# Third layer's mixer: gate and value pairs projected first, convolution ahead of queries and keys, taps between attention steps

## Chip, core and metric

The kernel runs on one core of one Trainium2 chip. The time is the device time of one execution in microseconds (us), from the first to the last instruction of the program. TensorE does the matrix products and writes to PSUM (eight banks); ScalarE, VectorE read PSUM and work on SBUF; SyncE issues the weight transfers. The trace calls them PE (with PEld for the loading of stationary operands), ACT, DVE and SP.

## What is computed

Three transformer layers run one after the other on 256 positions of width 1024, all in float32. The first two are of one kind and are not touched. The third is this, cut to what matters:

```python
def hybrid_mixer(h, w_in, b_f, conv_w, conv_b, conv_ln_g, conv_ln_b, w_o):
    proj = h @ w_in                       # q 512, k 512, v 512, f 8, value 512, gate 512
    log_f = jax.nn.log_sigmoid(f_logit + b_f)
    attn = fox_attention(q, k, v, log_f)  # 8 heads; logits + cum[t] - cum[s], causal softmax
    u = conv_val * jax.nn.sigmoid(conv_gate)
    u = causal_depthwise_conv(u, conv_w, conv_b)      # 31 taps, 512 channels
    u = jax.nn.silu(layer_norm(u, conv_ln_g, conv_ln_b))
    return jnp.concatenate([attn, u], axis=-1) @ w_o

    # around it: mod = silu(c) @ ada_w + ada_b gives shift, scale and gate (sh, sc, g) of mixer and FFN
    #   h = rms_norm(x, pre_g) * (1 + sc) + sh;  x = x + g * rms_norm(mixer or FFN of h, post_g)
```

## The kernel before

**Units.** All weights pass through one list, `UNITS`. A unit is 1 MB of weights: 256 output columns of a projection (for `f`, 128 columns). SyncE loads it into one of six `raw` buffers; ScalarE copies it, rounded, to `w_hi`; VectorE subtracts to get `w_lo` (the split, three buffers each); TensorE then makes three products for each pair of blocks (hi by hi, lo by hi, hi by lo), 48 matmuls of 256 columns for a unit. The split of unit m waits until unit m-3 is done on TensorE. ScalarE and VectorE each walk the list by hand: `step()` moves to the next unit, `split_ahead()` splits the one three further on, `tick()` does both, `unit_in()` waits until TensorE is done with the unit at hand. All engines run their instructions strictly as the code is written; semaphores (`Event`, `wait_ge`) tie them together.

**PSUM.** Results of units go to four banks in rotation (`plan_banks`), and a unit waits until the bank's last user has been evacuated by ScalarE or VectorE. Four more banks (`A`, "steps" in the trace) hold attention, sums and the FFN's output.

**Third layer.** The first two units, `gate0` and `val0`, are multiplied with the not yet normalised x (`x_shifted`) and scaled when VectorE evacuates them (`shifted_evac`); the reciprocal root `rs` comes from `norm_sum(4)` and ScalarE. Then `normalise(4)` on VectorE and `normed_hi(4)` on ScalarE make `h_hi` and `h_lo` for all other units. `modulation(1)`, 24 products of one column each (48 matmuls in the trace), makes the last three vectors of `mod`; its results are needed for `gain` from the end of the mixer on. The units followed as f, q0, q1, k0, k1, v0, v1, gate1, val1, out0 to out3, then the FFN's: gate, up and down in turn.

**Convolution.** Of its four chunks of 128 channels, 0 to 2 are done on VectorE tap by tap (`conv(taps, chunks)`, 31 taps, `conv_acc` in the trace), chunks 0 and 1 in alternation and chunk 2 alone. Chunk 3 is done on TensorE by 31 matmuls with diagonal matrices (`last_chunk`, 62 in the trace), which ScalarE builds (`diagonals(n)`, eight at a time). Chunks 0 and 1 need gate0 and val0; 2 and 3 need gate1 and val1.

**Attention** goes in two blocks of 128 queries, `first` and `second`, generators that are advanced with `next`: logits on TensorE, maxima on VectorE (`row_max`), exponentials on ScalarE (`probs`), transposes of `probs` on TensorE, copies on ScalarE (`probsT`), products with v, scaling to `y_tm` on VectorE, transposes again, and the split into `ya_hi` and `ya_lo`. Their logits wait for all of k and for `c_rows`, the running sums of the forget gate.

**FFN start.** `feed_forward(2)`: gate unit 0 and up unit 0 are again multiplied with `x_shifted` and evacuated with `shifted_evac`; gate unit 1 takes the bank that gate unit 0 had.

## Time and profile before

| | |
|---|---|
| median of 3 executions | 1255.02 us (1252.8 to 1255.05) |
| the profiled execution | 1247.75 us, span 1246.0 us |
| TensorE busy | 1172.1 us, 94% of the span, mean granted clock 0.975 |
| VectorE busy | 846.0 us, 68% |
| ScalarE busy | 614.9 us, 49% |
| DMA | 214.15 MB, mean 172 GB/s |
| third layer's mixer (from its first unit) | 872.95 to about 1021 us |

TensorE's share is an average: it is nearly full in the FFNs and has its idle pieces between the stages. The whole change lies between 880 and 1066 us of the span.

### The profile page before, as it was taken

How to read it: one execution, taken by the hardware profiler on the slowest of the kernel's cores; microseconds unless marked ns; L12 is line 12 of the kernel's file. 1: busy time of each engine (PE TensorE's matmuls, PEld its weight loads, DVE VectorE, ACT ScalarE, POOL GpSimd, SP SyncE). 2: the span in 40 equal slices, each digit the busy share in tenths (PEclk: the TensorE clock that was granted, in tenths of full speed). 3: DMA queues.
4: the chain of work that ended last, by engine and by line, in shares of the span. 5: the costliest groups of instructions: out<-in, count | busy, mean ns of one | idle time of the engine just before them, and what ended most of it. 6: DMA issues, size and time to landing. Idle time of an engine off the chain costs nothing.

```text
span 1246.0 us, 21102 instructions
## 1 busy us (share of the span) xinstructions
PE 1172.1 (94%) x9014; PEld 1135.4 (91%) x9014; DVE 846.0 (68%) x1270; ACT 614.9 (49%) x738; POOL 0.2 (0%) x4
## 2 busy tenths in 40 slices
PE   5999999999999999999999999999989787999996
PEld 4799899999999988999899999999889687999996
DVE  6995565777686779946567776768596747444453
ACT  7675347454433365653465534333594365433433
POOL 0000000000000000000000000000000000000000
PEclk9999999999999989999999999999799898999998
DMA  9446343747676744543347378867353122555511
GB/s 346 149 153 199 107 135 102 244 162 259 231 262 233 271 140 135 172 152 119 101 136 250 125 269 270 281 228 222 98 182 102 56 102 73 178 190 171 195 42 34
DMA packets 177614, 214.15 MB, mean 172 GB/s; under 512 B 3696, under 2 KB 160752, under 8 KB 177520
## 3 DMA queue, kind: packets, MB, share of 16 engines
q1 hardware_dynamic: 176800, 211.86, 51.4%
q8 instruction: 71, 1.16, 0.4%
q10 hardware_dynamic: 720, 0.94, 0.2%
q14 instruction: 23, 0.19, 0.0%
HBM read 211.74 MB, written 1.05 MB: 171 GB/s over the span
## 4 chain that ended last, share of the span: by engine, by line
PE 70%; DVE 17%; ACT 9%; issue 2%; DMA 1%; SPq 0%; DVEq 0%; ACTq 0%
PE stream L494 15%; PE stream L495 15%; PE stream L496 15%; DVE w_lo L1341 7%; PE steps L496 4%; PE steps L495 4%; PE steps L494 4%; ACT w_hi L907 4%; PE steps L825 2%; PE steps L683 1%; PE stream L702 1%; PE stream L608 1%; DMA raw<-in_w_in 1%; DVE score L1478 1%; PE steps L673 1%
## 5 line engine op out<-in xcount | busy, mean ns | idle before, releaser
L1341 DVE TENSOR_TENSOR w_lo<-raw,w_hi 128x2048 fp32r<-128x2048 f32 (+2 forms) x178 | 402.5, 2266 | 253.5 <-ACT w_hi L907 252.7
L907 ACT ACTIVATE w_hi<-raw 128x2048 fp32r<-128x2048 f32 (+2 forms) x178 | 336.4, 1893 | 357.8 <-PE stream L496 315.3
L494 PE MATMUL stream<-h_hi,w_hi 128*128 128x256 f32 x1576 | 451.1, 286 | 13.3 <-DVE w_lo L1341 9.5
L495 PE MATMUL stream<-h_lo,w_hi 128*128 128x256 f32 x1576 | 447.6, 284 | 0.0
L496 PE MATMUL stream<-h_hi,w_lo 128*128 128x256 f32 x1576 | 447.5, 284 | 0.0
L494 PEld LDWEIGHTS stream<-h_hi,w_hi 128*128 128x128 f32 x1576 | 304.1, 193 | 16.0 <-DVE w_lo L1341 11.0
L495 PEld LDWEIGHTS stream<-h_lo,w_hi 128*128 128x128 f32 x1576 | 304.2, 193 | 0.6 <-issue 0.5
L496 PEld LDWEIGHTS stream<-h_hi,w_lo 128*128 128x128 f32 x1576 | 303.9, 193 | 0.0
L494 PE MATMUL steps<-gu_hi,w_hi 128*128 128x256 f32 x528 | 149.6, 283 | 0.7 <-DVE gu_lo L1601 0.7
L496 PE MATMUL steps<-gu_hi,w_lo 128*128 128x256 f32 x528 | 149.5, 283 | 0.0
L495 PE MATMUL steps<-gu_lo,w_hi 128*128 128x256 f32 x528 | 149.5, 283 | 0.0
L494 PEld LDWEIGHTS steps<-gu_hi,w_hi 128*128 128x128 f32 x528 | 101.4, 192 | 0.9 <-issue 0.9
L496 PEld LDWEIGHTS steps<-gu_hi,w_lo 128*128 128x128 f32 x528 | 101.4, 192 | 0.0
L495 PEld LDWEIGHTS steps<-gu_lo,w_hi 128*128 128x128 f32 x528 | 101.4, 192 | 0.0
L1553 DVE SCALAR_TENSOR_TENSOR ada_sum<-ada_raw,c_act,ada_sum 128x256 f32<-128x256 f32 x168 | 81.5, 485 | 6.0
L907 ACT ACTIVATE gu_hi<-gu 128x512 fp32r<-128x512 f32 x33 | 20.9, 632 | 102.0 <-DVE gu L1597 98.0
L569 PE MATMUL stream<-w_hi,x_gained_hi 128*128 128x512 f32 (+1 forms) x96 | 37.6, 392 | 13.7 <-DVE w_lo L1341 12.4
L1868 DVE SCALAR_TENSOR_TENSOR conv_acc<-conv_in,params,conv_acc 128x256 f32<-128x256 f32 x90 | 39.1, 481 | 1.1
L1601 DVE TENSOR_TENSOR gu_lo<-gu,gu_hi 128x512 fp32r<-128x512 f32 x33 | 22.9, 693 | 23.0 <-ACT gu_hi L907 23.0
L907 ACT ACT_TABLE_LOAD x27 | 34.6, 1283 | 5.1 <-DMA xT<-in_x 4.6
L494 PE MATMUL stream<-x_gained_hi,w_hi 128*128 128x256 f32 x128 | 36.6, 286 | 0.0
L495 PE MATMUL stream<-x_gained_lo,w_hi 128*128 128x256 f32 x128 | 36.2, 283 | 0.0
(286 smaller groups left out, 1651.9 us busy)
## 6 DMA issues: line engine op xcount, KB each, us to landing
raw<-in_w_ffn_in SPq DMA_DIRECT2D x66, 1024.0 KB, 5.2
raw<-in_w_in SPq DMA_DIRECT2D x54, 1024.0 KB, 5.7
raw<-in_w_ffn_out SPq DMA_DIRECT2D x33, 1024.0 KB, 7.6
ada_raw<-in_ada_w SPq DMA_DIRECT2D x24, 1024.0 KB, 5.3
raw<-in_w_out SPq DMA_DIRECT2D x8, 1024.0 KB, 5.0
raw<-in_w_proj_attn SPq DMA_DIRECT2D x8, 512.0 KB, 3.5
raw<-in_w_proj_hgrn SPq DMA_DIRECT2D x8, 512.0 KB, 4.5
raw<-in_w_o SPq DMA_DIRECT2D x4, 1024.0 KB, 4.9
```

The source lines that it names most:

```text
L494: pe.matmul(dst, w_h, x_h, start=start, stop=False, skip_group_check=True)
L495: pe.matmul(dst, w_h, x_l, start=False, stop=False, skip_group_check=True)
L496: return pe.matmul(dst, w_l, x_h, start=False, stop=stop, skip_group_check=True)
L569: pe.matmul(dst, h_h[:, k0 + k, ts], hi[:, k, :], start=k0 + k == 0, stop=False)
L608: mm = pe.matmul(S[ada_bank[b]][:, j:j + 1], ada_sum[:, j // 2, P * (j % 2):P * (j % 2) + P], ones[:, 0:1], start=True, stop=True)
L673: mm = pe.transpose(B[n_t // 4][:, P * (n_t % 4):P * (n_t % 4) + P], pr[:, h, P * s:P * s + P], ident)
L825: mm = pe.matmul(pair_bank(i, g)[:, c - 2 * g, t, :], hk[:, c, P * t:P * t + P], qp[:, c, P * tq:P * tq + P], start=True, stop=True)
L907: return act.activation(out_, in_, func, **kw)
L1341: tt(wl[m % SPL][:, 0:n], raw[m % RAW][:, 0:n], wh[m % SPL][:, 0:n].bitcast(F32), ALU.subtract)\
L1553: ins = stt(acc, w[:, k, :], cact[:, k:k + 1], acc, ALU.mult, ALU.add)
L1601: tt(gu_l[i % 2].rearrange("p c t -> p (c t)"), gu, gu_h[i % 2].rearrange("p c t -> p (c t)").bitcast(F32), ALU.subtract).then_inc(*lane.m ...
L1868: ins = stt(cv[:, c, :], src, w, cv[:, c, :], ALU.mult, ALU.add)
```

## The change

1. Order of units: f, gate1, val1, q0, q1, k0, k1, v0, v1. So both chunk pairs of the convolution's input are known before queries and keys.
2. TensorE: `modulation(1)` goes behind val0 and writes to `A[1]` instead of a bank of the rotation, so it doesn't wait for gate0's evacuation; its evacuation on VectorE and the making of `gain` go behind seven taps of the convolution. TensorE waits for it before the first logits.
3. TensorE: `last_chunk` becomes a generator of four pieces of 8, 8, 8 and 7 taps that go between the steps of the attention.
4. VectorE: the first taps begin right behind val0; all 31 taps of chunks 0 and 1 and four of chunk 2 now stand ahead of the first maxima, the others of chunk 2 between attention steps.
5. ScalarE: the gate's sigmoid follows f, the rows for f are written before q0 is evacuated, evacuations go ahead of splits and diagonals, the last diagonals go behind the first exponentials.
6. VectorE, FFN of the third layer: gate unit 0 is evacuated before `normalise(5)`, and the split that stood behind `normalise(5)` and ahead of that evacuation stays behind `normalise(5)`.

The diff, without the hunks that only name the new event `values_set` (`v_set`), the new bank `ada_bank = (S[...], A[1])` and the wait of the second layer's unit:

```diff
@@ -96,9 +96,9 @@
     for name, w, kind in (("gate0", V_GATE, "fm"), ("val0", V_VAL, "fm"), ("f", V_F, "fm"),
+                          ("gate1", V_GATE + UC, "fm"), ("val1", V_VAL + UC, "fm"),
                           ("q0", V_Q, "fm"), ("q1", V_Q + UC, "fm"), ("k0", V_K, "fm"), ("k1", V_K + UC, "fm"),
-                          ("v0", V_V, "tm"), ("v1", V_V + UC, "tm"),
-                          ("gate1", V_GATE + UC, "fm"), ("val1", V_VAL + UC, "fm")):
+                          ("v0", V_V, "tm"), ("v1", V_V + UC, "tm")):
         units.append((kind, 2, name, w, UC if name != "f" else P))
@@ -601,11 +601,12 @@
 
-            for e, c in BANKS[ada_unit[b]][1]:
-                pe.wait_ge(evac[e], c)
+            if b == 0:
+                for e, c in BANKS[ada_unit][1]:
+                    pe.wait_ge(evac[e], c)
             pe.wait_ge(ada_summed, ADA_LAYER * (b + 1))
             for j in range(2 * ADA_LAYER):
-                mm = pe.matmul(S[ada_bank[b]][:, j:j + 1], ada_sum[:, j // 2, P * (j % 2):P * (j % 2) + P], ones[:, 0:1],
+                mm = pe.matmul(ada_bank[b][:, j:j + 1], ada_sum[:, j // 2, P * (j % 2):P * (j % 2) + P], ones[:, 0:1],
                                start=True, stop=True)
@@ -698,9 +699,12 @@
                 if j % 8 == 0:
+                    if j:
+                        yield
                     pe.wait_ge(*c_diag.at(0, j // 8))
                 mm = pe.matmul(conv_bank[:, 0:T], diag[j], upad[:, 3, j:j + T], start=j == 0, stop=j == CONV_K - 1)
             mm.then_inc(c_tap.sem, 1)
+            yield
 
@@ -856,12 +860,14 @@
         norm_sum(4)
+        stream(1)
         modulation(1)
-        stream(1)
-        stream(5, normed(4))
+        stream(7, normed(4))
         pe.wait_ge(*c_rows.at(0))
+        pe.wait_ge(*ada_out.at(0, 1))
         first = attend(2, 0, [evacuated(unit(2, "k1"))])
         second = attend(2, 1, [a_pte.at(2, 1)])
+        taps = last_chunk()
         next(first)
@@ -869,11 +875,12 @@
         next(first)
-        stream(1)
+        next(taps)
         next(first)
-        stream(1)
+        next(taps)
         next(second)
-        last_chunk()
+        next(taps)
+        next(taps)
         next(second)
@@ -1268,34 +1270,36 @@
         f(lfa, lfa, ACT.Ln, bias=1.0).then_inc(*lane.mark(c_f))
+        tick()
+        unit_in()
+        act.wait_ge(*v_set.at(0))
+        f(sgate, b2(here()), ACT.Sigmoid).then_inc(*emptied())
+        tick()
         act.wait_ge(ada_done, 2)
         f(qa[DH:DH + H], ident[DH:DH + H, DH:DH + H].unsqueeze(2).broadcast_to([H, H, T]), ACT.Copy).then_inc(*lane.step())
+        act.wait_ge(*c_cum.at(0))
+        f(ka[DH:DH + H], lfa.unsqueeze(1).broadcast_to([H, H, T]), ACT.Copy, scale=-1.0 / SCALE).then_inc(*lane.mark(c_rows))
+        act.wait_ge(*n_lo.upto(4))
         for i, dst in enumerate((qa, ka)):
             for j in range(2):
-                tick()
+                step()
                 unit_in()
                 for n in range(2):
                     ins = f(dst[0:DH, 4 * j + n:4 * j + 4:2, :], b2(here())[DH * n:DH * n + DH], ACT.Copy)
                     ins.then_inc(*(emptied() if n else lane.step()))
-                if i and j:
-                    act.wait_ge(*n_lo.upto(4))
-                diagonals(2 * i + j)
-                if (i, j) == (0, 1):
-                    act.wait_ge(*c_cum.at(0))
-                    f(ka[DH:DH + H], lfa.unsqueeze(1).broadcast_to([H, H, T]), ACT.Copy, scale=-1.0 / SCALE)\
-                        .then_inc(*lane.mark(c_rows))
+                split_ahead()
+                if not (i and j):
+                    diagonals(2 * i + j)
         first, second = attend(2, 0), attend(2, 1)
         next(first)
+        diagonals(3)
         for j in range(2):
             tick()
             unit_in()
             f(v[:, :, UC * j:UC * j + UC], b2(here()), ACT.Copy).then_inc(*emptied())
             if j == 0:
                 next(first)
-        act.wait_ge(*evacuated(unit(2, "val0")))
-        value_gate()
         next(first)
-        tick()
         next(second)
@@ -1558,15 +1562,15 @@
                 dve.wait_ge(ada_done, 1)
-            if b == 2:
-                normalise(5, lambda k: gain[:, 1, k:k + 1], lambda k: mod[:, 3, k:k + 1])
             for i in range(FS):
-                tick()
+                step()
                 late = scaled_after(UNITS[here()])
                 shift = shifted(UNITS[here()])
                 if shift:
                     dve.wait_ge(*n_rs.at(5))
                     shifted_evac(sg[i].rearrange("p (c t) -> p c t", c=2), 0, True)
+                    normalise(5, lambda k: gain[:, 1, k:k + 1], lambda k: mod[:, 3, k:k + 1])
+                split_ahead()
                 if late:
@@ -1844,16 +1848,8 @@
         split_ahead()
-        modulation(1)
         dve.memset(upad[:, :, 0:CONV_K - 1], 0.0).then_inc(*lane.step())
-
         ts_(vis, vis, -NEG, None, ALU.add).then_inc(*lane.step())
-        dve.wait_ge(ada_out.sem, 2)
-        ts_(gain[:, 1, :], mod[:, 4, :], 1.0, None, ALU.add).then_inc(*lane.step())
-        tt(gain[:, 2, :], mod[:, 2, :], pc("mix_post", 0, 8), ALU.mult).then_inc(*lane.step())
-        tt(gain[:, 3, :], mod[:, 5, :], pc("ffn_post", 0, 8), ALU.mult).then_inc(*lane.step())
-        dve.wait_ge(*lane.last)
-        tt(gain[:, 1, :], gain[:, 1, :], pc("ffn_pre", 0, 8), ALU.mult).then_inc(*lane.mark(gains_set))
 
@@ -1868,15 +1864,24 @@
 
-        tick()
+        step()
         shifted_evac(cv[:, 2:4, :], 1, True)
         dve.wait_ge(*lane.last)
         dve.wait_ge(*v_sig.at(0))
         for c in range(2):
-            stt(upad[:, c, CONV_K - 1:PADW], cv[:, 2 + c, :], sbias[:, 1, c:c + 1], sgate[:, c, :], ALU.add, ALU.mult)\
-                .then_inc(*lane.step())
+            ins = stt(upad[:, c, CONV_K - 1:PADW], cv[:, 2 + c, :], sbias[:, 1, c:c + 1], sgate[:, c, :], ALU.add, ALU.mult)
+            ins.then_inc(*(lane.mark(v_set) if c else lane.step()))
         dve.wait_ge(*lane.last)
-        conv(range(0, 2), (0, 1))
+        conv(range(0, 1), (0, 1))
+        split_ahead()
+        conv(range(1, 7), (0, 1))
+        modulation(1)
+        dve.wait_ge(*lane.last)
+        ts_(gain[:, 1, :], mod[:, 4, :], 1.0, None, ALU.add).then_inc(*lane.step())
+        tt(gain[:, 2, :], mod[:, 2, :], pc("mix_post", 0, 8), ALU.mult).then_inc(*lane.step())
+        tt(gain[:, 3, :], mod[:, 5, :], pc("ffn_post", 0, 8), ALU.mult).then_inc(*lane.step())
+        dve.wait_ge(*lane.last)
+        tt(gain[:, 1, :], gain[:, 1, :], pc("ffn_pre", 0, 8), ALU.mult).then_inc(*lane.mark(gains_set))
         tick()
@@ -1890,31 +1895,36 @@
             dve.wait_ge(*lane.last)
-        conv(range(2, 4), (0, 1))
-        for n in range(3):
-            tick()
-            conv(range(4 + 4 * n, 8 + 4 * n), (0, 1))
+        conv(range(7, 10), (0, 1))
         tick()
-        first, second = (attend(2, qt, vis[:, T - P * (qt + 1):T]) for qt in range(NT))
-        next(first)
-        conv(range(16, 18), (0, 1))
-        tick()
-        conv(range(18, 22), (0, 1))
-        tick()
-        next(second)
-        next(first)
-        conv(range(22, 26), (0, 1))
-        tick()
-        next(first)
-        conv(range(26, CONV_K), (0, 1))
+        conv(range(10, 16), (0, 1))
         tick()
         unit_in()
         dve.wait_ge(*evacuated(here() - 1))
         tt(upad[:, 2:4, CONV_K - 1:PADW], bank(here()).rearrange("p (c t) -> p c t", c=2), sgate, ALU.mult)\
             .then_inc(*emptied())
+        conv(range(16, 20), (0, 1))
+        tick()
+        conv(range(20, 24), (0, 1))
+        tick()
+        conv(range(24, 28), (0, 1))
+        tick()
+        conv(range(28, CONV_K), (0, 1))
+        tick()
+        conv(range(0, 4), (2,))
+        first, second = (attend(2, qt, vis[:, T - P * (qt + 1):T]) for qt in range(NT))
+        next(first)
+        conv(range(4, 8), (2,))
+        tick()
+        conv(range(8, 14), (2,))
         next(second)
-        dve.wait_ge(*lane.last)
-        conv(range(CONV_K), (2,))
+        next(first)
+        tick()
+        conv(range(14, 20), (2,))
+        next(first)
+        conv(range(20, 24), (2,))
+        next(second)
+        conv(range(24, CONV_K), (2,))
         next(second)
```

VectorE ahead of the first attention maxima (`ISA probs,row_max`), before. `w_lo` rows are splits, `conv_acc` rows are taps (x8 is four taps of two chunks); the numbers behind names are buffers:

```order
L1868 SCALAR_TENSOR_TENSOR conv_acc<-conv_in,params,conv_acc 128x256 x4
L1341 TENSOR_TENSOR w_lo_59<-raw_53,w_hi_56 128x2048
L1868 SCALAR_TENSOR_TENSOR conv_acc<-conv_in,params,conv_acc 128x256 x8
L1341 TENSOR_TENSOR w_lo_60<-raw_54,w_hi_57 128x2048
L1868 SCALAR_TENSOR_TENSOR conv_acc<-conv_in,params,conv_acc 128x256 x8
L1341 TENSOR_TENSOR w_lo_58<-raw_49,w_hi_55 128x2048
L1868 SCALAR_TENSOR_TENSOR conv_acc<-conv_in,params,conv_acc 128x256 x8
L1341 TENSOR_TENSOR w_lo_59<-raw_50,w_hi_56 128x2048
L1498 ISA probs,row_max<-steps,consts 128x128
```

and now, from the product of value and gate of the second pair on:

```order
L1904 TENSOR_TENSOR conv_in<-stream,conv_gate 128x2x256
L1864 SCALAR_TENSOR_TENSOR conv_acc<-conv_in,params,conv_acc 128x256 x8
L1345 TENSOR_TENSOR w_lo_58<-raw_49,w_hi_55 128x2048
L1864 SCALAR_TENSOR_TENSOR conv_acc<-conv_in,params,conv_acc 128x256 x8
L1345 TENSOR_TENSOR w_lo_59<-raw_50,w_hi_56 128x2048
L1864 SCALAR_TENSOR_TENSOR conv_acc<-conv_in,params,conv_acc 128x256 x8
L1345 TENSOR_TENSOR w_lo_60<-raw_51,w_hi_57 128x2048
L1864 SCALAR_TENSOR_TENSOR conv_acc<-conv_in,params,conv_acc 128x256 x6
L1345 TENSOR_TENSOR w_lo_58<-raw_52,w_hi_55 128x2048
L1861 TENSOR_SCALAR conv_acc<-conv_in,params 128x256
L1864 SCALAR_TENSOR_TENSOR conv_acc<-conv_in,params,conv_acc 128x256 x3
L1502 ISA probs,row_max<-steps,consts 128x128
```

The product for the second pair has come here from behind the second block's first maxima, and the first four taps of chunk 2 (one tensor-scalar and three of `conv_acc`) and two more splits stand ahead of the first maxima: the last split ahead of them was that of the unit nine behind gate0, and is now that of the unit eleven behind it (out0).

TensorE around the first taps with a diagonal (`conv_diagonal_130`), before: they come behind gate1, val1 and the second half of the second block's logits:

```order
L496 MATMUL stream<-h_hi,w_lo_60 128x256
L663 MATMUL steps<-k_and_cum,q_and_pick 128x256 x4
L702 MATMUL stream<-conv_in,conv_diagonal_130 128x256
L702 MATMUL stream<-conv_in,conv_diagonal_131 128x256
L702 MATMUL stream<-conv_in,conv_diagonal_132 128x256
L702 MATMUL stream<-conv_in,conv_diagonal_133 128x256
L702 MATMUL stream<-conv_in,conv_diagonal_134 128x256
```

and now, behind the first half of these logits and the first block's product with v:

```order
L664 MATMUL steps<-k_and_cum,q_and_pick 128x256 x4
L684 MATMUL steps<-v,probsT 128x64 x8
L705 MATMUL stream<-conv_in,conv_diagonal_130 128x256
L705 MATMUL stream<-conv_in,conv_diagonal_131 128x256
L705 MATMUL stream<-conv_in,conv_diagonal_132 128x256
L705 MATMUL stream<-conv_in,conv_diagonal_133 128x256
L705 MATMUL stream<-conv_in,conv_diagonal_134 128x256
L705 MATMUL stream<-conv_in,conv_diagonal_135 128x256
L705 MATMUL stream<-conv_in,conv_diagonal_136 128x256
L705 MATMUL stream<-conv_in,conv_diagonal_137 128x256
L691 MATMUL steps<-consts,y_tm 128x128 x4
L705 MATMUL stream<-conv_in,conv_diagonal_138 128x256
```

The `y_tm` transposes of the first block, which had whole units ahead of them, now stand behind eight taps, and eight more taps follow.

VectorE at the start of the third layer's FFN, before (`silu_g_121` is gate unit 0's evacuation, `gu` that of up unit 0):

```order
L1413 SCALAR_TENSOR_TENSOR h_lo<-h_norm,mod,h_hi 128x256 x4
L1341 TENSOR_TENSOR w_lo_59<-raw_53,w_hi_56 128x2048
L1384 TENSOR_TENSOR silu_g_121<-stream,rstd 128x256 x2
L1386 COPY shift_product<-stream 128x1 x2
L1341 TENSOR_TENSOR w_lo_60<-raw_54,w_hi_57 128x2048
L1384 TENSOR_TENSOR gu<-stream,rstd 128x256 x2
```

and now:

```order
L1388 TENSOR_TENSOR silu_g_121<-stream,rstd 128x256 x2
L1390 COPY shift_product<-stream 128x1 x2
L1425 SCALAR_TENSOR_TENSOR h_norm<-xT,gain_186,rstd 128x256 x4
L1417 SCALAR_TENSOR_TENSOR h_lo<-h_norm,mod,h_hi 128x256 x2
L1425 SCALAR_TENSOR_TENSOR h_norm<-xT,gain_186,rstd 128x256 x2
L1417 SCALAR_TENSOR_TENSOR h_lo<-h_norm,mod,h_hi 128x256 x2
L1425 SCALAR_TENSOR_TENSOR h_norm<-xT,gain_186,rstd 128x256 x2
L1417 SCALAR_TENSOR_TENSOR h_lo<-h_norm,mod,h_hi 128x256 x4
L1345 TENSOR_TENSOR w_lo_59<-raw_53,w_hi_56 128x2048
L1345 TENSOR_TENSOR w_lo_60<-raw_54,w_hi_57 128x2048
L1388 TENSOR_TENSOR gu<-stream,rstd 128x256 x2
```

The evacuation of gate unit 0 has moved from behind the normalisation and a split to ahead of both.

## Rows read from the trace of the kernel before

**Rows 1.** The page, part 1: busy us, share of the span, instructions.

```profile
PE 1172.1 (94%) x9014; PEld 1135.4 (91%) x9014; DVE 846.0 (68%) x1270; ACT 614.9 (49%) x738; POOL 0.2 (0%) x4
```

**Rows 2.** TensorE's waits, 860 to 1060 us: total us, times, longest.

```profile
PE stream L494 <- DVE w_lo L1341: 6.3, 1, 6.3
PE steps L663 <- ACT k_and_cum L907: 5.0, 1, 5.0
PE stream L702 <- DVE conv_in L1913: 4.1, 1, 4.1
PE stream L886 <- ACT scratch L907: 2.4, 1, 2.4
```

**Rows 3.** Windows: busy us (instructions) of PE, PEld, DVE, ACT, POOL; granted clock; DMA.

```profile
931.00:937.00 6.00, 6.00 (x28) 6.00 (x29) 4.66 (x22) 3.36 (x15) 0.00 (x0) 0.50 0.54 175
976.00:986.00 10.00, 10.00 (x48) 8.76 (x47) 9.32 (x20) 0.26 (x2) 0.00 (x0) 1.00 0.00 0
996.30:1000.00 3.70, 3.68 (x24) 3.47 (x25) 0.69 (x2) 2.87 (x4) 0.00 (x0) 1.00 0.00 0
```

**Rows 4.** Timeline of TensorE: start, duration, operation, count, [idle before, releaser].

```profile
883.97 8.35 PE L608 MATMUL stream<-ones,ada_sum 128*128 128x1 f32 x48 [1.93 <-DVE shift_product L1386]
...
950.89 2.00 PE L683 MATMUL steps<-v,probsT 128*128 128x64 f32 x16 [0.81 <-ACT v L907]
...
964.71 1.89 PE L663 MATMUL steps<-k_and_cum,q_and_pick 72*128 72x256 f32 x8
...
986.29 1.91 PE L673 MATMUL steps<-consts,probs 128*128 128x128 f32 x16
```

**Rows 5.** Timeline of VectorE, 892 to 988 us.

```profile
892.92 0.18 DVE L1432 TENSOR_TENSOR mod<-stream,params 128x24 f32<-128x24 f32 x1
...
904.32 0.75 DVE L1384 TENSOR_TENSOR conv_acc<-stream,rstd 128x256 f32<-128x256 f32 x2
...
907.60 2.29 DVE L1341 TENSOR_TENSOR w_lo<-raw,w_hi 128x2048 fp32r<-128x2048 f32 x1
909.80 0.47 DVE L1884 TENSOR_SCALAR f_min<-stream,params 8x256 f32<-8x256 f32 x1
...
911.71 1.67 DVE L1868 SCALAR_TENSOR_TENSOR conv_acc<-conv_in,params,conv_acc 128x256 f32<-128x256 f32 x4
...
920.86 3.26 DVE L1868 SCALAR_TENSOR_TENSOR conv_acc<-conv_in,params,conv_acc 128x256 f32<-128x256 f32 x8
...
932.19 0.29 DVE L1498 CUSTOM_DVE_ANT_0 probs<-steps,consts 128x128 f32<-128x128 f32 x1 [0.28 <-PE steps L663]
...
935.29 0.17 DVE L1501 TENSOR_SCALAR row_max<-row_max 128x8 f32<-128x8 f32 x1
...
972.67 15.59 DVE L1868 SCALAR_TENSOR_TENSOR conv_acc<-conv_in,params,conv_acc 128x256 f32<-128x256 f32 x30
```

**Rows 6.** Timeline of ScalarE, 929 to 976 us.

```profile
929.61 1.21 ACT L907 ACTIVATE k_and_cum<-stream 64x512 f32<-64x512 f32 x2
...
938.51 0.19 ACT L907 ACTIVATION_READ_ACCUMULATOR probs<-probs,row_max 128x1 f32 x1
...
972.22 0.51 ACT L907 ACTIVATE probs<-probs,row_max 128x256 f32<-128x256 f32 x1 [4.03 <-DVE row_max L1501]
...
976.07 0.19 ACT L907 ACTIVATION_READ_ACCUMULATOR probs<-probs,row_max 128x1 f32 x1
```

**Rows 7.** Timeline of ScalarE at the third layer's FFN.

```profile
1047.05 1.89 ACT L907 ACTIVATE w_hi<-raw 128x2048 fp32r<-128x2048 f32 x1
...
1052.10 0.91 ACT L907 ACTIVATE silu_g<-silu_g,shift_product 128x256 f32<-128x256 f32 x2 [1.86 <-DVE shift_product L1386]
...
1060.35 1.91 ACT L907 ACTIVATE w_hi<-raw 128x2048 fp32r<-128x2048 f32 x1 [0.84 <-PE stream L496]
...
1066.11 1.91 ACT L907 ACTIVATE w_hi<-raw 128x2048 fp32r<-128x2048 f32 x1 [3.36 <-PE stream L496]
```

**Rows 8.** Timeline of VectorE there: `gu_lo` of the first unit.

```profile
1059.54 0.69 DVE L1601 TENSOR_TENSOR gu_lo<-gu,gu_hi 128x512 fp32r<-128x512 f32 x1 [0.70 <-ACT gu_hi L907]
```

More of the change, by code:

```diff
@@ L355, in build @@
     ada_out = Event("ada_evacuated")
-    ada_unit = (U0[1] + 4, U0[2] + 2)
-    ada_bank = [BANKS[m][0][0] for m in ada_unit]
+    ada_unit = U0[1] + 4
+    ada_bank = (S[BANKS[ada_unit][0][0]], A[1])
     gains_set = Event("gains_set")
@@ L382, in build @@
     c_diag, c_tap, c_pe = Event("diagonals_set", 4), Event("last_chunk_summed"), Event("last_chunk_set")
-    c_rows = Event("cum_rows_set")
+    c_rows, v_set = Event("cum_rows_set"), Event("values_set")
     c_f, c_cum, c_conv, c_ms, c_mu, c_cen, c_sq, c_var, c_rs, c_aff, c_act, c_hi, c_lo = (
@@ L537, in stream @@
                     pe.wait_ge(evac[e], c)
-                if m in ada_unit:
-                    pe.wait_ge(*ada_out.at(0, b - 1))
+                if m == ada_unit:
+                    pe.wait_ge(*ada_out.at(0, 0))
                 wait = dict(before or {})
@@ L1245, in _ @@
         rstd(rs, A[0][:, 0:T], D, n_ms.at(4), n_rs)
-        def value_gate():
-            tick()
-            unit_in()
-            f(sgate, b2(here()), ACT.Sigmoid).then_inc(*emptied())
         def diagonals(n):
@@ L1431, in modulation @@
             flat = mod.rearrange("p j c -> p (j c)")[:, n * b:n * b + n]
-            tt(flat, S[ada_bank[b]][:, 0:n], pc("ada_b", n * b, n), ALU.add).then_inc(*lane.mark(ada_out))
+            tt(flat, ada_bank[b][:, 0:n], pc("ada_b", n * b, n), ALU.add).then_inc(*lane.mark(ada_out))
         def rotate(x, n, cos, sin):
@@ L1892, in _ @@
             dve.wait_ge(*lane.last)
-        conv(range(2, 4), (0, 1))
-        for n in range(3):
-            tick()
-            conv(range(4 + 4 * n, 8 + 4 * n), (0, 1))
+        conv(range(7, 10), (0, 1))
         tick()
-        first, second = (attend(2, qt, vis[:, T - P * (qt + 1):T]) for qt in range(NT))
-        next(first)
-        conv(range(16, 18), (0, 1))
-        tick()
-        conv(range(18, 22), (0, 1))
-        tick()
-        next(second)
-        next(first)
-        conv(range(22, 26), (0, 1))
-        tick()
-        next(first)
-        conv(range(26, CONV_K), (0, 1))
+        conv(range(10, 16), (0, 1))
         tick()
```

## The prediction, made before the changed kernel ran

> **What bounds the kernel now.** I read the page first: TensorE is busy for 94% of the span [rows 1], so only a place where it waits or runs at its lower clock can give time back. The second view, TensorE's waits, names the places between 860 and 1060 us [rows 2]: 5.0 us ahead of the first logits (for k1's evacuation), 4.1 us ahead of the taps with a diagonal (for the last product into `conv_in`), 6.3 us ahead of gate unit 1 of the FFN. The releaser named for the last is a split, but the work due is what follows it on VectorE, the evacuation of gate unit 0, whose bank gate unit 1 takes. The modulation's own row shows 1.9 us more, for gate0's evacuation [rows 4]. Third, the granted clock [rows 3]: after the 5.0 us wait it is 0.50, the 1.2 GHz level, and 28 matmuls take 6.0 us, 0.214 us each. At the full level a unit of 48 takes 5.76 us, read off two ScalarE splits that TensorE released, at 1060.35 and 1066.11 [rows 7], so 0.120 us each. A microsecond at the lower level thus loses 0.44 us. Last, the timelines of VectorE and ScalarE give durations.
>
> **VectorE up to the first maxima.** Up to 892.92, where the split of the unit three behind gate0 has ended [rows 5], nothing changes but the unit's name. From there VectorE's order has, up to the first `row_max`:
> - memset, mask, modulation's evacuation and gains: seven small ones, the first 0.18 us [rows 5]; I take 0.9 us together.
> - val0's evacuation and product, the first tap pair and one more: from 904.32 to 907.60, 3.3 us [rows 5].
> - the forget gate's part: 909.80 to 911.71, 1.9 us [rows 5].
> - 29 more taps of two chunks, 58 instructions. Eight take 3.26 us [rows 5], so 0.40 us each with their overlap: 23.2 us.
> - eight splits (val1, q0, q1, k0, k1, v0, v1, out0), 907.60 to 909.80 or 2.2 us each [rows 5]: 17.6 us.
> - the second pair's product, on 128x512 elements, some 0.7 us; four taps of chunk 2, alone, 15.59/30 = 0.52 us each [rows 5]: 2.1 us.
> - eight maxima: before from 932.19 to 935.46, 3.3 us with waits for logits [rows 5]; without them I take 2.2 us.
>
> The sum is 51.9 us; with about 0.6 us of waits for ScalarE's copies the maxima are set at 945.4. Before they were set at 935.46, with 15 taps fewer done. The exponentials took from there to 938.70, 3.2 us [rows 5, 6]; they now end at 948.6.
>
> **TensorE up to the same point.** Before, the matmuls of k1 ended at about 926.0 (logits released when the evacuation of 929.61 ends at 930.82, less the 5.0 us) [rows 2, 6]. Now gate1 and val1 lie ahead of it (2 x 5.76) and the 1.9 us wait is gone, since val0 needs no bank that gate0 holds: 935.6. The modulation itself moves at the same price, 8.35 us with its time at the lower clock [rows 4]. ScalarE has the new order with evacuations first and two units more time, so the logits wait only for k1's evacuation, 1.2 us [rows 6]: 936.8. Logits 2 us, v0 5.8 us: 944.6. Then the transposes of `probs` wait until 948.6. **So the 5.0 us wait shrinks to 1.2 and a new one of 4.0 us arises, behind VectorE, which has become the bound of this stretch.** Queued behind the waiting transposes are v1, the product with v and all taps.
>
> Does the clock fall in it? After the 5.0 us wait it had [rows 3]; behind the 2.4 us ahead of the sums over `scratch`, at 996.3, it is still 1.00 [rows 2, 3]. 4.0 us is nearer to the former, so I take a fall and some 4.5 us at the lower level after it: 2.0 us lost (bounds 0 and 2.6, all 6.0 us of the row). The Trainium skill, "TensorE: Matmul & The Clock Gate", section "HAM oscillation — how this bites in real kernels", says the same of a wait of this kind: bursts of matmuls with waits between them start again at half the clock every time. By that rule the loss stands; by the row at 996.3 the sum would be 2.0 us better.
>
> **Behind it.** Transposes 1.0 (half of 1.91 [rows 4]) and v1 5.8, with the clock loss: 957.4. ScalarE's split and v1's evacuation 2.5: 959.9; product with v 2.0 [rows 4]: 961.9. Taps: 48 matmuls of them in 10.0 us [rows 3], 0.21 each; the 62 come to 13.0 us (before 15.7 with the lower clock behind the 4.1 us wait). Eight taps 3.4, transposes of `y_tm` 0.4, eight more 3.4: 969.1. The second half of the second block's logits needs `ya_lo`: VectorE has `y_tm` at 962.6, a split 2.2, six taps 3.1, `ya_lo` 0.7, so 968.6, in time. Logits 1.9 [rows 4], 15 taps 6.3: 977.3. The other side: maxima end at 972.3, exponentials take 4.0 us (972.22 to 976.26 [rows 6]) and end at 976.4. So the second block's transposes start at 977.3 instead of 986.29 [rows 4]: **9.0 us**. What follows up to the out units has the same order on all engines and waits for these same things; chunk 2's taps end before it, so they are hidden as before.
>
> **FFN.** Up unit 0 ended 6.3 us ahead of 1052.16, at 1045.8. Gate unit 0's evacuation now comes first and frees the bank in time; it delays the normalisation by 1.0 us. Its pairs of `h_lo` are then due up to 1049.0, and gate unit 1 takes its pairs in order until 1051.6. Up unit 1 waits for its split: ScalarE 1047.05 [rows 7] + 1.0 + 1.9, VectorE 2.3: 1052.2, ends 1058.0. Down unit 0 needs `gu_lo`, which was ready at 1060.2 [rows 8]. ScalarE's silu waited 1.86 us for the evacuation [rows 7] and no longer does, against 1.0 us of delay: 1059.3. Down unit 0 started when up unit 1 ended, just ahead of 1066.1 [rows 7], so at 1066.0; it now starts at 1059.4: **6.6 us** (bounds 5.7, with `gu_lo` no earlier, and 8.0, with no wait). From there on both run unit by unit, and the moved DMAs, one load for each unit in the same ring of six, start with the splits, all of which are at or ahead of their old times.
>
> **Sum.** 9.0 + 6.6 = 15.6 us off the profiled execution's 1247.75 (span 1246.0 and 1.75 around it): 1232.1. The median of the runs, 1255.02, lies 7.3 us above that execution; I take the difference off the median: **1239.4 us**, 1.2% faster. No change by measurement would be within 0.2%, 2.5 us.
>
> **Rivals.**
> - *VectorE costs more than its sum* (chance 0.12). If tap pairs at work beside a full TensorE take the single price, 0.52 us, 58 of them add 7.0 us, all of it in the new wait. The mixer gives 2.0 and the FFN 6.6: 1246.4. For it speaks that VectorE has no gap left in 51 us; against it, the eight in 3.26 us ran beside busy units.
> - *The lower clock stays* (0.04), the slower side. From 948.6 to the out units TensorE has some 32 us of full-speed work in short bursts; at 0.214 for 0.120 all of it costs 25 us, 23 more than counted: 1262. It decides from about 20 us of that work on. Against it: between 976 and 986, in taps, the clock was 1.00 [rows 3]. The section of the Trainium skill's TensorE page named above is what would make it so, if each short wait counted.
> - *The gain is given back* (0.04): if the FFN's loads set its pace, an earlier start waits there, and 1255 stays. Against it: between 860 and 1060 none of the listed waits is for a load, and up units end one unit time apart.
> - *As forecast* (0.80), its own range 1233 to 1243: without the fall of the clock 1237.4, with a modulation that keeps the full clock longer and the FFN at 8.0 about 1235; with the FFN at 5.7 and a clock loss of 2.6, 1241; 2 us for the runs' own spread.
>
> The range for 8 in 10 reaches into the first rival: 1232 to 1247. Faster 0.91, same 0.04, slower 0.05.
>
> **What would show it.** TensorE's wait ahead of the modulation gone; a wait of 1 to 2 us ahead of the first logits; one of about 4 us ahead of the first `probs` transposes, with VectorE busy without a gap from 890 to 945 us and clock 0.50 behind it; no wait of 4 us ahead of the taps; second transposes near 977; in the FFN gate unit 1 right behind up unit 0, and waits of under 2 us ahead of up unit 1 and down unit 0. It would be wrong if VectorE's stretch came to much over 52 us, or if ScalarE's longer chain (sigmoid, q0, k0 and diagonals) made a split late that VectorE then waits for.

## The result, and the profile after

The changed kernel takes 1231.2 us (median of 4 runs, 1230.6 to 1231.9), beside it the kernel before 1253.9 us (4 runs, 1250.8 to 1255.05): ratio on record 0.984, 95% interval 0.981 to 0.987, so 1.6% faster (the two medians alone give 0.982). One run of the kernel before, in a later round, took 1302.96 us at a mean granted clock of 0.833; it is a slow run and is left out everywhere. The profiled execution took 1230.79 us (span 1229.0), 17.0 us less than that of before. Forecast were 1239.4 us for the median and 1232.1 us for the profiled execution; the range of 1232 to 1247 lies just above the measured median.

The page of the changed kernel, part 1 (against [rows 1]):

```profile
PE 1163.5 (95%) x9014; PEld 1127.7 (92%) x9014; DVE 845.0 (69%) x1270; ACT 614.6 (50%) x738; POOL 0.2 (0%) x4
```

TensorE's waits between 860 and 1060 us of the changed kernel (total us, times, longest):

```profile
PE stream L494 <- DVE x_shifted_lo L1398: 8.0, 2, 5.4
PE steps L674 <- ACT probs L914: 6.1, 1, 6.1
PE stream L893 <- ACT scratch L914: 2.4, 1, 2.4
PE steps L494 <- DVE gu_lo L1605: 1.9, 2, 1.2
PE steps L664 <- ACT k_and_cum L914: 1.4, 1, 1.4
PE steps L684 <- ACT v L914: 0.8, 1, 0.8
PE stream L494 <- DVE w_lo L1345: 0.6, 1, 0.6
```

Of the waits in [rows 2] the 5.0 us ahead of the logits are 1.4, and the 4.1 us ahead of the taps and the 6.3 us ahead of gate unit 1 of the FFN are gone, as is the 1.9 us ahead of the modulation [rows 4]. The 0.6 us still put down to `w_lo` stand one unit later, ahead of up unit 1. A new one of 6.1 us stands ahead of the transposes of `probs`: the one that was forecast, at 4.0.

TensorE's timeline of the changed kernel (against [rows 4]; start, duration, operation, count, wait):

```profile
887.50 5.41 PE L609 MATMUL steps<-ones,ada_sum 128*128 128x1 f32 x48
...
933.32 2.02 PE L664 MATMUL steps<-k_and_cum,q_and_pick 72*128 72x128 f32 x16 [1.39 <-ACT k_and_cum L914]
...
947.24 1.97 PE L674 MATMUL steps<-consts,probs 128*128 128x128 f32 x8 [6.14 <-ACT probs L914]
...
958.29 2.00 PE L684 MATMUL steps<-v,probsT 128*128 128x64 f32 x16 [0.82 <-ACT v L914]
960.13 3.67 PE L705 MATMUL stream<-conv_in,conv_diagonal 128*128 128x256 f32 x16
963.64 0.60 PE L691 MATMUL steps<-consts,y_tm 128*128 128x128 f32 x4
964.07 3.62 PE L705 MATMUL stream<-conv_in,conv_diagonal 128*128 128x256 f32 x16
...
975.74 1.91 PE L674 MATMUL steps<-consts,probs 128*128 128x128 f32 x16
...
1041.61 0.39 PE L494 MATMUL stream<-h_hi,w_hi 128*128 128x256 f32 x1 [0.56 <-DVE w_lo L1345]
...
1048.82 0.35 PE L494 MATMUL steps<-gu_hi,w_hi 128*128 128x256 f32 x1 [1.20 <-DVE gu_lo L1605]
```

The second block's transposes start at 975.74 instead of 986.29, 10.5 us earlier, and down unit 0 (the last row) at 1048.82 instead of 1065.85 (read from TensorE's timeline of before), 17.0 us earlier. So all of the gain is made by then: 10.5 us in the mixer and 6.5 in the FFN's start.

VectorE's timeline of the changed kernel (against [rows 5]):

```profile
892.86 0.16 DVE L1851 MEMSET conv_in<- 128x120 f32 x1
892.93 0.23 DVE L1852 TENSOR_SCALAR consts<-consts 128x256 f32<-128x256 f32 x1
893.08 0.74 DVE L1388 TENSOR_TENSOR conv_acc<-stream,rstd 128x256 f32<-128x256 f32 x2
...
919.40 3.25 DVE L1864 SCALAR_TENSOR_TENSOR conv_acc<-conv_in,params,conv_acc 128x256 f32<-128x256 f32 x8
...
943.78 0.17 DVE L1505 TENSOR_SCALAR row_max<-row_max 128x8 f32<-128x8 f32 x1
```

and ScalarE's behind it (against [rows 6]):

```profile
943.99 0.40 ACT L914 ACTIVATE probs<-probs,row_max 128x128 f32<-128x128 f32 x1 [7.71 <-DVE row_max L1505]
...
946.99 0.19 ACT L914 ACTIVATION_READ_ACCUMULATOR probs<-probs,row_max 128x1 f32 x1
```

No row of VectorE between 892.86 and 943.95 shows idle time ahead of it; ScalarE waits 7.7 us for the maxima, and TensorE 6.1 us for ScalarE. That is the chain to read: the engine named in TensorE's wait is ScalarE, but the work that was late stands one step further back, on VectorE.

### The profile page after: what moved, and what is told of

The parts are those of the page before. It is cut to its first block, busy times and chain, and to the rows that moved or that the text cites. A ratio compares the mean times of both kernels' runs of the same rounds, so it can differ in the third digit from the quotient of the medians.

```text
span 1229.0 us, 21102 instructions
## 1 busy us (share of the span) xinstructions
PE 1163.5 (95%) x9014; PEld 1127.7 (92%) x9014; DVE 845.0 (69%) x1270; ACT 614.6 (50%) x738; POOL 0.2 (0%) x4
## 4 chain that ended last, share of the span: by engine, by line
PE 69%; DVE 19%; ACT 7%; issue 3%; DMA 1%; SPq 0%; DVEq 0%; ACTq 0%
PE stream L494 15%; PE stream L496 15%; PE stream L495 15%; DVE w_lo L1345 7%; PE steps L494 5%; PE steps L496 4%; PE steps L495 4%; ACT w_hi L914 3%; PE steps L829 2%; PE steps L684 1%; PE stream L705 1%; DMA raw<-in_w_in 1%; DVE conv_acc L1864 1%; ACT probs L914 1%; DVE score L1482 1%
## 5 line engine op out<-in xcount | busy, mean ns | idle before, releaser
L569 PE MATMUL stream<-w_hi,x_gained_hi 128*128 128x512 f32 (+1 forms) x96 | 37.7, 392 | 13.4 <-DVE w_lo L1345 12.1
```

The lines of the kernel that those rows point to most:

```text
L569: pe.matmul(dst, h_h[:, k0 + k, ts], hi[:, k, :], start=k0 + k == 0, stop=False)
```

## Experiments

In each I read two stretches of TensorE as well as the total: **A**, from the first matmul of `norm_sum(4)`, right behind `gate0`, to the second block's transposes of `probs`, and **B**, from there to down unit 0. (Theory A in the expectations is a name of a theory, not this stretch.) The last three columns are where A begins, which is where `gate0` ends, how long `gate0` took, and how long the modulation took.

| profiled execution | A | B | total | A begins | gate0 | modulation |
|---|---|---|---|---|---|---|
| before; again (e7) | 106.1; 106.1 | 79.6; 79.5 | 1247.75; 1247.55 | 880.15; 880.03 | 7.2; 7.1 | 8.35; 8.43 |
| changed; again (e8) | 95.7; 95.7 | 73.1; 73.1 | 1230.79; 1230.21 | 880.03; 879.47 | 7.1; 7.1 | 5.41; 5.41 |
| old FFN order (e1) | 95.7 | 79.6 | 1236.95 | 879.74 | 7.1 | 5.41 |
| new FFN order alone (e2) | 109.7 | 73.2 | 1243.91 | 879.01 | 5.8 | 7.8 |
| modulation moved alone (e9) | 103.6 | 79.5 | 1248.01 | 882.98 | 5.8 | 7.6 |
| modulation back (e5) | 102.6 | 73.1 | 1237.42 | 879.78 | 7.1 | 8.4 |
| four more taps ahead of the maxima (e6) | 97.7 | 73.0 | 1233.82 | 881.13 | 8.55 | 6.76 |
| maxima ahead of chunk 2 (e10) | 94.7 | 74.5 | 1232.37 | 881.26 | 7.2 | 5.41 |
| maxima behind v1's split (e3; e11) | 92.4; 92.5 | 74.2; 74.1 | 1230.18; 1232.98 | 881.63; 884.50 | 5.8; 5.8 | 7.8; 7.9 |
| taps in one piece (e4) | 104.2 | 72.6 | 1241.77 | 883.04 | 5.8 | 7.9 |

The code ahead of A is the same in all of them, and yet A begins up to 5.5 us apart; the last experiment comes back to that. `gate0` too is the same work behind the same wait of 2.7 us, and took 5.8 us at the full clock or 7.1 and more with part of it at the lower one. The modulation, where it stands behind val0 with no wait ahead, goes the other way: 5.4 us where `gate0` took 7.1 or 7.2 (four profiles), 7.6 to 7.9 where it took 5.8 (four). So A is not free of the clock: between profiles whose `gate0` differs, the modulation alone puts up to 2.5 us into A, and up to 1.3 us of that were saved ahead of A. Where it matters I also count from the start of `gate0`: 102.85 us to the second block's transposes in the changed kernel, 113.3 in the kernel before.

### The FFN's order, undone and alone

In `feed_forward(2)` on VectorE; the first run takes this out of the changed kernel, the second puts it alone into the kernel before:

```diff
-            if b == 2:
-                normalise(5, lambda k: gain[:, 1, k:k + 1], lambda k: mod[:, 3, k:k + 1])
             for i in range(FS):
-                tick()
+                step()
...
                     shifted_evac(sg[i].rearrange("p (c t) -> p c t", c=2), 0, True)
+                    normalise(5, lambda k: gain[:, 1, k:k + 1], lambda k: mod[:, 3, k:k + 1])
+                split_ahead()
```

> The changed kernel with one part taken back: at the third layer's FFN VectorE normalises and splits before it evacuates gate unit 0, as before. Theory A (the two gains stand apart and add up): TensorE waits 6.3 us for that evacuation ahead of gate unit 1 and runs 4.6 us at the lower clock behind it, so the profiled execution is 6.7 us longer than that of the changed kernel (1230.8), 1237.5. Rival B (the FFN's part is hidden, the whole gain is the mixer's): within 1 us of 1230.8.

> The kernel before with that part of the change alone: gate unit 0 evacuated before the normalisation. Theory A: 6.7 us off the 1247.75 of the profiled execution before, 1241.0. Rival B: within 1 us of 1247.75.

Undone: 1236.95 us (4 runs, 1236.8 to 1241.3), 6.2 us more than the changed kernel's profiled execution. Alone: 1243.86 us (4 runs, 1242.35 to 1245.6), ratio to before 0.994 (0.992 to 0.996). The wait in the first, from TensorE's waits of the same stretch:

```profile
PE stream L494 <- DVE w_lo L1345: 6.4, 1, 6.4
```

B is 79.6 us with the old order and 73.1 or 73.2 with the new, in either mixer: the term is worth 6.4 to 6.5 us and adds to the mixer's. The total of the run with it alone shows only 3.8 us against 1247.75, of 6.7 expected, because its stretch A took 3.6 us more than that of before, with the same waits ahead of TensorE. More of its work ran at the lower clock: the first block's product with v took 3.1 us instead of 2.0, and `gate1` behind it 8.1 instead of 6.0.

### Where VectorE takes the maxima

The first run takes the maxima right behind v1's split, the second puts four more taps of chunk 2 ahead of them, the third takes them ahead of chunk 2's four:

```diff
-        conv(range(28, CONV_K), (0, 1))
-        tick()
-        conv(range(0, 4), (2,))
         first, second = (attend(2, qt, vis[:, T - P * (qt + 1):T]) for qt in range(NT))
         next(first)
-        conv(range(4, 8), (2,))
+        conv(range(28, CONV_K), (0, 1))
+        tick()
+        conv(range(0, 8), (2,))
```

```diff
-        conv(range(0, 4), (2,))
+        conv(range(0, 8), (2,))
...
         next(first)
-        conv(range(4, 8), (2,))
```

```diff
-        conv(range(0, 4), (2,))
...
         next(first)
-        conv(range(4, 8), (2,))
+        conv(range(0, 8), (2,))
```

> The changed kernel with the first block's maxima moved on VectorE from behind out0's split and four taps of chunk 2 to right behind v1's split; these taps, the last three tap pairs and the split follow the maxima. Theory A (VectorE's order ahead of the maxima bounds the stretch, TensorE's 6.1 us wait ahead of the first probs transposes is its price): the maxima start at 935.5 instead of 942.0, the exponentials end ahead of v0's end at 941.1, the wait and the fall of the clock with it go, and the work that was moved fits into the 5.2 us in which VectorE then waited for a split. The second block's transposes start at about 968.3 instead of 975.7: 7.4 us off, 1223.4. Rival C (the next wait in line, ScalarE's copies, diagonals and splits, is due at nearly the same time): the wait moves to the products with v or to the taps and no more than 2 us come off, 1229 to 1231.

> The changed kernel with four more taps of chunk 2 on VectorE ahead of the first maxima instead of behind them. Theory A (VectorE bounds the stretch up to the first maxima): four taps by 0.52 us put the maxima 2.1 us later, the wait ahead of the first transposes of probs becomes 8.2 us, and all behind it moves by 2.1 us: 1233 us. Rival (TensorE or ScalarE bounds the stretch, or the slack behind the wait takes it): no change, within 0.7 us of 1231.

> The changed kernel with VectorE's first maxima ahead of the four taps of chunk 2 that stand in front of them, a smaller step of the same kind as the maxima behind v1's split. Theory A (VectorE sets the end of the first maxima): they end 2.1 us earlier (51.1 us after VectorE's w_lo split of the unit three behind gate0 becomes 49.0), the wait ahead of the first transposes shrinks from 6.1 to 4.1, and the whole takes 1228.5 profiled, if the clock does not do something else. Rival C (the lower clock behind the wait or VectorE's later taps take it back): 1230 to 1231.

The first transposes, read off TensorE's timeline, with four more taps (one row) and ahead of chunk 2 (the other):

```profile
950.42 1.54 PE L674 MATMUL steps<-consts,probs 128*128 128x128 f32 x6 [6.62 <-ACT probs L914]
```

```profile
946.58 1.97 PE L674 MATMUL steps<-consts,probs 128*128 128x128 f32 x8 [4.25 <-ACT probs L914]
```

Counted from the start of A they begin after 69.3 us with four more, 65.3 us with four fewer, and 67.2 in the changed kernel: 2.1 us later and 1.9 us earlier, as VectorE's bound says, and the second block's transposes follow by 2.0 and 1.0. In the wait itself only 0.5 us of the 2.1 show, since the modulation took 6.8 us instead of 5.4 and brought TensorE there later. In the total, four more cost 3.0 us (1.1 of them ahead of A), and four fewer gave nothing (1232.37): A began 1.2 us later, v1 took 0.9 us more behind the wait, and the sums behind the 2.4 us wait 1.5 us more. So theory A held for the place, and rival C for the total. By the medians, 1236.9 us (4 runs, 1233.8 to 1238.3) and 1232.2 us (4 runs, 1231.7 to 1235.4).

With the maxima behind v1's split the wait is gone and none takes its place:

```profile
PE stream L494 <- DVE x_shifted_lo L1398: 8.0, 2, 5.4
PE stream L893 <- ACT scratch L914: 2.4, 1, 2.4
PE steps L494 <- DVE gu_lo L1605: 1.9, 2, 1.2
PE steps L664 <- ACT k_and_cum L914: 1.4, 1, 1.4
PE steps L684 <- ACT v L914: 0.8, 1, 0.8
PE stream L494 <- DVE w_lo L1345: 0.6, 1, 0.6
```

A fell by 3.3 us, of 7.4 forecast, since now VectorE waits 1.6 us for the logits and TensorE sets the pace; there the modulation took 7.8 us (5.4), v0 7.2 (6.0). In both profiles of this kernel `gate0` took 5.8 us, so part of this is the clock's pattern and not the edit: from the start of `gate0` they gain 4.6 us. And the total stayed at 1230.55 us (5 runs, 1225.3 to 1232.0): in the profiled one A began 1.6 us later and B took 1.1 us more.

### The place of the modulation

Back ahead of val0 in the changed kernel:

```diff
         norm_sum(4)
+        pe.wait_ge(*evacuated(unit(2, "gate0")))
+        modulation(1)
         stream(1)
-        modulation(1)
```

and behind val0 in the kernel before, with the bank `A[1]` as in the change, VectorE's evacuation of it behind val0's product and two taps, and TensorE's wait for that ahead of the first logits:

```diff
         norm_sum(4)
-        modulation(1)
         stream(1)
+        modulation(1)
         stream(5, normed(4))
```

> The changed kernel with TensorE's modulation back ahead of value unit 0 and behind gate0's evacuation, as it was in the kernel before; nothing else is undone. Theory A (VectorE's order of work sets the end of the first maxima, TensorE has 6.1 us to spare there): the modulation costs TensorE the wait of about 1.9 us ahead of it, and may take up to 2.9 us more at the lower clock, but the wait ahead of the first transposes of probs shrinks from 6.1 us by as much. The second block's transposes start within 0.5 us of where they did, counted from the start of the layer's first unit (102.85 us), and the whole is within 1.5 us of the changed kernel. Rival: the place of the modulation is worth what it shows on TensorE, so the whole is 1.9 to 4.9 us slower.

> The kernel before, with one edit of the change: TensorE's modulation behind value unit 0 (in bank 1 of the attention steps), and VectorE's evacuation of it behind value unit 0's product. Theory V (what the place of the modulation is worth lies in when value unit 0 ends, since VectorE's stretch starts with its evacuation; in the old order VectorE bounds nothing up to the first logits): TensorE saves the wait of 1.9 us and up to 2.9 us of low clock, and this is all that can come through, 1.9 to 4.9 us, less what the 5.0 us wait for k1's evacuation grows by if ScalarE is late there. I expect 2 to 4 us off 1247.7 profiled, 1244 to 1246. Rival 1 (the wait of 5.0 us takes all of it): 1247 to 1248, and a wait of 7 to 10 us ahead of the first logits. Rival 2 (VectorE's earlier start is worth the 6.6 us in the old order as well): about 1241, with the 4.1 us wait ahead of the taps gone too.

Back: 1240.5 us (6 runs, 1237.4 to 1246.75), A 6.9 us longer. **My theory was wrong here.** I had counted TensorE's spare 6.1 us as room for it, but the wait shrank by 0.5 only. VectorE's timeline of this run says why, and TensorE's the cause:

```profile
892.59 0.16 DVE L1852 MEMSET conv_in<- 128x120 f32 x1
892.66 0.23 DVE L1853 TENSOR_SCALAR consts<-consts 128x256 f32<-128x256 f32 x1
899.76 0.76 DVE L1389 TENSOR_TENSOR conv_acc<-stream,rstd 128x256 f32<-128x256 f32 x2 [6.86 <-PE stream L496]
```

```profile
883.60 8.43 PE L609 MATMUL steps<-ones,ada_sum 128*128 128x1 f32 x48 [1.93 <-DVE shift_product L1391]
```

VectorE's bound stretch begins with val0's evacuation. With the modulation ahead of it val0 ends so late that VectorE idles 6.9 us, and everything up to the maxima moves by that. In the changed kernel val0 ended at 887.7, 5.2 us before VectorE was free. The spare 6.1 us on TensorE lie behind val0; ahead of it there were only the 5.2 us by which it ended early. Val0 ends some 12.1 us later: 1.9 us of wait, 8.3 of modulation, and 1.7 that val0 itself takes longer at the lower clock. Had both run at the full clock (5.3 and 5.8 us, as in the changed kernel), it would have been 7.2 us, 2.0 beyond the 5.2 by this estimate. So most of the 6.9 us, nearly 5, is the lower clock behind the 1.9 us wait, carried to VectorE by the place.

Moved alone in the old order: 1247.4 us (10 runs, 1244.05 to 1249.3), ratio 0.997 (0.995 to 0.999), A 2.5 us shorter: the 1.9 us wait, and 7.6 us for the modulation instead of 8.35. The 5.0 us wait stays at 4.8 and the 4.1 us wait stays, which rules out both rivals, though the profiled total, 1248.01, lies where rival 1 had it: A began 2.8 us later. So the same edit is worth 2.5 us of A in the old order and 6.9 in the new. Part of this contrast is the clock's pattern (`gate0` 5.8 us here, 7.1 in both profiles of the new order); from the start of `gate0` it is 3.9 against 6.9.

### The taps in one piece

```diff
-        next(taps)
...
-        next(taps)
...
+        for _ in range(4):
+            next(taps)
```

> The changed kernel with the 31 taps of chunk 3 on TensorE in one piece again, behind the second half of the second block's logits. Theory A: interleaving them covers TensorE's waits for y_tm and ya_lo; without it TensorE waits 0.8 us ahead of the y_tm transposes and some 5 us ahead of the logits' second half (VectorE's split and six taps stand between y_tm and ya_lo), with perhaps a fall of the clock behind it: 5 to 8 us longer, 1236 to 1239. Rival D (the taps' place is neutral, since VectorE and ScalarE set the pace): within 1.5 us of 1230.8.

1244.15 us (4 runs, 1241.8 to 1246.9). A is 8.5 us longer than in the changed kernel, somewhat over the 5 to 8 expected (7.2 from the start of `gate0`), and another 3.0 us of the total stand ahead of it. TensorE's timeline:

```profile
969.02 3.78 PE L664 MATMUL steps<-k_and_cum,q_and_pick 72*128 72x256 f32 x8 [4.68 <-DVE ya_lo L1516]
972.60 14.77 PE L705 MATMUL stream<-conv_in,conv_diagonal 128*128 128x256 f32 x62
```

Without taps between them the attention's steps wait for each other, 4.7 us ahead of these logits and 0.9 ahead of the transposes of `y_tm`; and behind the wait the logits take 3.8 us instead of 1.9.

### Both kernels and the one without the wait, once more

> The kernel before, unchanged, profiled once more, since its first profiled execution took 1247.75 us and its timed runs 1249 to 1255 us. Theory P (executions differ only by where TensorE's clock falls, by some us): this profile has the same list of waits ahead of TensorE to within 1 us in all, and its span differs from the first by what the modulation and other stretches at the lower clock take more or less; timed runs with the same granted clock have the same span to within 1.5 us. Rival: a wait for a transfer or for another engine comes and goes, and would show as a difference of over 2 us in the list of waits.

> The changed kernel, unchanged, profiled once more beside the kernel before again on the same chip. Theory P: 1231 +/- 2 us, modulation 5.4 to 7.9 us, the wait ahead of the first transposes of probs smaller by what the modulation is dearer, so that the second block's transposes start within 1 us of 102.85 us after the start of the layer's first unit. Rival: the start of the transposes moves with the modulation's time, by up to 2.4 us.

> The kernel with the first maxima right behind v1's split, unchanged, timed once more with more rounds. Theory P (the wait is gone in every run, and the runs differ by where the clock falls): runs with a granted clock of 0.984 lie at 1225 to 1226 and runs with 0.977 to 0.979 at 1230 to 1232, and the profile has the same short list of waits as the first time. Rival (the 1225 us run was a chance of measurement): all runs within 1 us of 1230.5, or clock and time do not go together.

Before: 1251.6 us (10 runs, 1247.55 to 1256.8), profiled 1247.55, the list of waits the same to 0.1 us. Changed: 1233.6 us (4 runs, 1230.2 to 1238.5), profiled 1230.21, again the same list. Its modulation took 5.41 us, so the rival that the start of the transposes follows it had nothing to show itself on. The run with the taps in one piece decides it, whose code is the same up to there: with a modulation of 7.9 us and v0 at 7.2 instead of 6.0 the wait ahead of the first transposes shrank from 6.1 to 1.7 us, and they started 67.5 us behind the start of A instead of 67.2. They follow VectorE, not the modulation. Without the wait: 1231.1 us (6 runs, 1223.9 to 1236.5), profiled 1232.98, once more with the short list of waits.

Sorted by each run's mean granted clock, all runs that list it: before takes 1247.1 to 1250.0 us at 0.975, 1249.75 to 1253.6 at 0.971 and 0.972, and 1253.3 to 1256.8 at 0.967 to 0.970. The changed kernel takes 1230.2 to 1232.2 at 0.983 and 1235.0 and 1238.5 at 0.976. Without the wait it takes 1223.9, 1224.0 and 1225.3 at 0.984, 1230.2 to 1233.0 at 0.977 to 0.979, and 1236.5 at 0.973. The 1.5 us that I had given to runs of one clock were too narrow. Where the low clock falls goes with 8 to 13 us from one execution to the next. The windows of the changed kernel and of the one without the wait, in code that is the same in both (columns: us, busy time and count of PE, PEld, DVE, ACT, POOL, granted clock, DMA share, GB/s):

```profile
400.00:500.00 100.00, 98.28 (x648) 90.67 (x647) 83.39 (x140) 51.09 (x64) 0.00 (x0) 0.97 0.53 172
```

```profile
400.00:500.00 100.00, 98.26 (x635) 90.43 (x634) 81.24 (x139) 48.74 (x62) 0.00 (x0) 0.95 0.51 167
```

With the same busy time 13 matmuls fewer were done, and the third layer began at 878.67 instead of 872.89; TensorE's waits up to there agree within 0.7 us. Rank the two versions by like clock and the one without the wait is 6 us faster (1223.9 to 1225.3 against 1230.2 to 1232.2), but it had that clock in 3 of its 11 runs only, the changed kernel in 6 of 8; by the medians they cannot be told apart. Why an execution takes the one pattern or the other was not found.

## Why the prediction was right in its steps, and where its numbers were off

- **VectorE as the new bound: right.** Forecast 945.4 for the maxima, measured 943.95; 51.1 us from 892.86 on, where 51.9 and 0.6 of waits were summed. Pairs of taps cost 3.25 us for eight, as in [rows 5]; the 0.6 us of waits did not come, the maxima took 1.97 us instead of 2.2. The rival with dearer taps is out. The runs with taps moved confirm it from both sides (2.1 us later, 1.9 us earlier).
- **The modulation at the same price: wrong, and at first sight without effect.** 8.35 us were kept [rows 4]; it took 5.41. That was luck in part: at the same place, with no wait ahead, it took 7.6 to 7.9 us in four other profiles. TensorE came to `probs` 3.5 us earlier (941.1, forecast 944.6) and waited 6.1 us instead of 4.0. What its place was worth was not named at all as a step: VectorE's start at 892.92 rested on val0 ending before that. It did, and without it 6.9 us of the gain are lost (e5), nearly 5 of them through the lower clock behind the 1.9 us wait.
- **The lower clock behind the new wait: right, in size as well.** In the changed kernel the eight transposes took 1.97 us instead of 1.04 (without the wait) and v1 6.88 instead of 5.99, 1.8 us lost against 2.0 forecast:

```profile
944.90:951.00 6.10, 3.77 (x18) 3.77 (x19) 0.97 (x2) 6.10 (x20) 0.00 (x0) 0.51 0.00 0
960.00:976.00 16.00, 16.00 (x80) 14.04 (x80) 13.22 (x30) 4.70 (x18) 0.00 (x0) 1.00 0.19 66
```

  The Trainium skill, "TensorE: Matmul & The Clock Gate", section "HAM oscillation — how this bites in real kernels", says that matmuls behind such a wait start at half the clock. The traces agree for waits of 4.3 to 6.6 us ahead of these transposes (1.97 us for the eight, five variants); behind 1.7 us (e4) they took 1.09. But the rival built on it, that it stays low through the short bursts, did not happen: the second row shows 1.00 through taps, transposes and logits.
- **The mixer's term: 9.0 forecast, 10.5 measured.** Transposes of `probs` 1.4 us earlier than said (947.24 against 948.6) carried through; taps cost 13.5 us (start to next start) instead of 13.0, the logits' second half was in time, as said. How the term splits among the edits stays open in part: undone one at a time, the modulation's place costs 6.9 us and the taps' interleaving 8.5, together more than A's whole gain of 10.4, so they do not add up; the new order of units and that of ScalarE were never run alone.
- **The FFN's term: 6.6 forecast, 6.5 measured** (e1, e2). Both short waits are there, 0.56 and 1.20 us, where [rows 7, 8] had put 0.6 and about 1.4.
- **The sum: 15.6 forecast, 17.0 between the profiled executions, 17.3 between the repeated ones.** The median missed by 8.2 us, of which 1.3 are the sum. The rest is the step from the profiled execution to the median: I added 7.3 us, which the first three runs of before had above its profiled one. The changed kernel's runs lie 0.4 us above theirs in the first measurement and 3.4 in the second. That offset was no constant of the kernel but the share of its runs with a lower clock, and it does not carry from one kernel to another. It is what put the median 0.8 us below the range.

## What to carry to other kernels

Find the instruction that starts the bound engine's stretch, and ask what was moved ahead of it or behind it: an edit that only seems to fill idle time on TensorE was worth 6.9 us because it released val0 earlier to VectorE, and 2.5 to 3.9 us where VectorE was not the bound. Reckon spare time from a point in the program: the 6 us of slack behind val0 were of no use ahead of it, where there were 5.2 us and the edit took 12.1, much of it through the lower clock. When runs of one kernel spread by 7 us and more, compare stretches between fixed instructions, and look at the clock's pattern in each: three kernels profiled twice repeated A to 0.1 us, but each pair had the same pattern, and where it differed A moved by up to 3.6 us. Forecast the profiled execution and the spread apart.
